# Sixty-four of 128 rows of an adaLN product moved from the merge, projection and FFN stages into the gate units

## What is computed

```python
shift_mix, scale_mix, gate_mix, shift_ffn, scale_ffn, gate_ffn = jnp.split(
    silu_c @ w_ada[l] + b_ada[l], N_ADA, axis=-1)
...
h_x = modulate(x, norm_mix[l], shift_mix, scale_mix)
p_x = h_x @ w_in[l]
u_x, hy_x, gates_x = jnp.split(p_x, [S5_WIDTH, S5_WIDTH + 3 * HY_WIDTH], axis=-1)
y_x = (s5_readout(s5_states(u_x, lp, 0, st_ctx_f[:, -1], False), lp, 0)
       + s5_readout(s5_states(u_x, lp, 1, st_ctx_b[:, 0], True), lp, 1))
x = x + gate_mix[:, None] * mixer_output(u_x, y_x, hy_x, gates_x, lp)
x = x + gate_ffn[:, None] * swiglu(modulate(x, norm_ffn[l], shift_ffn, scale_ffn),
                                   w_ffn_in[l], w_ffn_out[l])
...
return rms_norm(x, norm_f)
```

## Time and profile before

| quantity | value |
|---|---|
| median of 3 runs | 2881.26 us (2880.14 to 2881.98) |
| span of the profiled execution | 2886.0 us |
| busy: PE, PEld, DVE | 2822.8, 2456.8, 1939.7 us |
| busy: ACT, POOL | 970.0, 272.1 us |
| gate units 10 to 31 | about 665 to 968 us |
| spectrum, merge, output projection | about 968, 1130 and 1311 us on, to 1474 us |
| FFN with its pairs, down projection | about 1482 to 2382 us, to 2866 us |

### The profile page before, as it was taken

One profiled execution on the slowest core, in us unless ns is written; L12 is line 12 of the kernel. 1 busy time (PEld: TensorE's weight loads), 2 busy tenths in 40 slices (PEclk: granted clock), 3 DMA queues, 4 the chain that ended last, 5 costly groups with the idle time before them and its releaser, 6 DMA issues.

```text
span 2886.0 us, 40851 instructions
## 1 busy us (share of the span) xinstructions
PE 2822.8 (98%) x17044; PEld 2456.8 (85%) x17044; DVE 1939.7 (67%) x2657; ACT 970.0 (34%) x1376; POOL 272.1 (9%) x475
## 2 busy tenths in 40 slices
PE   7999999999999999999989999999999999999997
PEld 2688788888888888887879999999999997888886
DVE  6546666985543777887768888888888774343445
ACT  4332333224442532221154444444443442222221
POOL 0001331001223001111100000000000000000000
PEclk9999999999999999999999999999999999999998
DMA  9726974334445537886544444444443335434333
GB/s 403 294 92 150 189 182 141 119 121 134 133 129 173 200 132 255 291 287 249 205 157 150 143 147 141 148 139 149 140 143 111 121 129 193 137 99 136 96 100 109
DMA packets 139531, 473.73 MB, mean 164 GB/s; under 512 B 24417, under 2 KB 24673, under 8 KB 134610
## 3 DMA queue, kind: packets, MB, share of 16 engines
q1 hardware_dynamic: 84226, 302.96, 31.8%
q0 software_dynamic: 47248, 156.09, 16.8%
q10 hardware_dynamic: 7872, 12.06, 1.2%
HBM read 426.53 MB, written 44.43 MB: 163 GB/s over the span
## 4 chain that ended last, share of the span: by engine, by line
PE 90%; DMA 4%; DVE 3%; ACT 2%; issue 1%; POOL 0%; ACTq 0%; DVEq 0%; SPq 0%; POOLq 0%
PE ps L2048 11%; PE ps L2050 10%; PE ps L2049 10%; PE ps L2303 10%; PE ps L2304 10%; PE ps L2305 10%; PE ps L2333 5%; PE ps L2334 5%; PE ps L2335 5%; DMA hw_raw<-in_w_in 2%; PE ps L2065 2%; PE ps L2018 1%; PE ps L2127 1%; DMA hw_raw<-in_w_out 1%; PE ps L2066 1%; PE ps L1959 1%
## 5 line engine op out<-in xcount | busy, mean ns | idle before, releaser
L1124 DVE TENSOR_TENSOR hw_lo<-hw_raw,hw_hi 128x1024 fp32r<-128x1024 f32 (+1 forms) x348 | 382.7, 1101 | 629.7 <-ACT hw_hi L680 628.0
L680 ACT ACTIVATE hw_hi<-hw_raw 128x1024 fp32r<-128x1024 f32 (+1 forms) x348 | 333.7, 961 | 1049.1 <-DMA hw_raw<-in_w_in 469.0
L1050 ACT ACTIVATE wx_hi<-wx 128x1024 fp32r<-128x1024 f32 x287 | 303.5, 1058 | 445.9 <-PE ps L2305 431.6
L1771 DVE TENSOR_TENSOR wx_lo<-wx,wx_hi 128x1024 fp32r<-128x1024 f32 x287 | 350.4, 1222 | 58.8 <-ACT wx_hi L1050 58.7
L2303 PE MATMUL ps<-t_hi,wx_hi 128*128 128x256 f32 x1312 | 371.3, 283 | 0.0
L2304 PE MATMUL ps<-t_lo,wx_hi 128*128 128x256 f32 x1312 | 371.3, 283 | 0.0
L2305 PE MATMUL ps<-t_hi,wx_lo 128*128 128x256 f32 x1312 | 371.3, 283 | 0.0
L2048 PE MATMUL ps<-h_hi,hw_hi 128*128 128x512 f32 x896 | 354.4, 396 | 3.7 <-DVE st_b L1389 2.6
L2050 PE MATMUL ps<-h_hi,hw_lo 128*128 128x512 f32 x896 | 350.6, 391 | 0.0
L2049 PE MATMUL ps<-h_lo,hw_hi 128*128 128x512 f32 x896 | 350.4, 391 | 0.0
L2303 PE MATMUL ps<-h_hi,wx_hi 128*128 128x256 f32 x984 | 278.6, 283 | 0.0
(11 more groups left out here) (359 smaller groups left out, 5187.6 us busy)
## 6 DMA issues: line engine op xcount, KB each, us to landing
wx<-in_w_fi SPq DMA_DIRECT2D x164, 512.0 KB, 3.3
hw_raw<-in_w_in SPq DMA_DIRECT2D x128, 512.0 KB, 4.2
ada1m<-in_w_ar POOLq DMA_DIRECT2D x128, 512.0 KB, 4.8
ada_mix<-in_w_ac SPq DMA_DIRECT2D x16, 2048.0 KB, 12.7
hw_raw<-in_w_fo SPq DMA_DIRECT2D x64, 384.0 KB, 3.1
hw_raw<-in_w_fo SPq DMA_DIRECT2D x64, 320.0 KB, 2.9
hw_raw<-in_w_glu SPq DMA_DIRECT2D x32, 512.0 KB, 4.8
hw_raw<-in_w_out SPq DMA_DIRECT2D x32, 512.0 KB, 4.4
```

What stands on the lines that cost most here:

```text
L680: act.activation(hw_hi[slot(n)][:, 0:width(n)], hw_raw[slot(n)][:, 0:width(n)], ACT.Copy).then_inc(w_hi, 1)
L1124: tt(hw_lo[s][:, 0:w], hw_raw[s][:, 0:w], hw_hi[s][:, 0:w].bitcast(F32), SUB).then_inc(w_lo, 1)
L1771: tt(wx_lo[o % 12][:, :], wx[o % 12][:, :], wx_hi[o % 4][:, :].bitcast(F32), SUB).then_inc(w_lo, 1)
```

## The change

Rows 0 to 63 (groups 0 to 3) are now added up in gate units 10 to 28, in the place of the first chunks of the S5 states, which nobody reads any more after the scan. They have three load buffers `ada1g` in place of four, and an accumulator in two pieces of 512 columns, so each row is two DVE instructions. Units 10 to 13 take four rows each, 14 to 17, 19 to 22 and 24 to 27 three, 18, 23 and 28 four. The sums over partitions of groups 0 to 3 stand on TensorE after H0 of units 14, 19, 24 and 29. Rows 64 to 127 stay in the merge (3 a full tile, 1 a filling tile, 36 in all) and in the output projection (2 a tile, 28 in all). The FFN has none.

```diff
-N_WIDE = 96
+N_GATE = 64
...
+    ada1g = [at(f"ada1g_{j}", 126 + 4 * j, [P, 1024]) for j in range(3)]
+    accg = [at(f"accg{j}", (138, 180)[j], [P, 512]) for j in range(2)]
...
+    def gate_rows(g):
+
+        if g < P3 or g >= P3 + 19:
+            return range(0)
+        if g < P3 + 4:
+            return range(4 * (g - P3), 4 * (g - P3) + 4)
+        q, i = (g - P3 - 4) // 5, (g - P3 - 4) % 5
+        return range(16 * q + 16 + 3 * i, 16 * q + 16 + (3 * i + 3 if i < 4 else 16))
...
             def ada_in(r):
 
-                if r >= 4:
-                    pool.wait_ge(ada1_used, r - (3 if r < N_WIDE + 2 else 1))
-                pool.dma_start(ada1m[row_slot(r)][:, :], w_ar_d[r]).then_inc(ada1_in[row_slot(r)], 16)
+                if 3 <= r < N_GATE:
+                    pool.wait_ge(ada1_used, r - 2)
+                if r >= N_GATE + 4:
+                    pool.wait_ge(ada1_used, r - 3)
+                pool.dma_start(row_buffer(r)[:, :], w_ar_d[r]).then_inc(ada1_in[row_slot(r)], 16)
...
+            pool.wait_ge(rec_dn, 1)
+            for r in range(3):
+                ada_in(r)
+            for r in gate_rows(P3):
+                ada_in(r + 3)
             for t in range(NS):
                 toeplitz(t)
+                for r in gate_rows(P3 + 1 + t):
+                    ada_in(r + 3)
                 if t == 9:
                     store_y(0)
+            for g in range(P3 + 1 + NS, P3 + 19):
+                for r in gate_rows(g):
+                    if r + 3 < N_GATE:
+                        ada_in(r + 3)
...
             store_y(1)
+            pool.wait_ge(ada1_used, N_GATE)
+            pool.wait_ge(acc1_red, 4)
             for s in range(2):
                 pool.dma_start(tf_raw[:, s, :, :], ...
...
@@ DVE, gate unit g
                 if 0 <= g - P3 - 2 < NS:
                     outputs(g - P3 - 2)
+                if g in (P3 + 4, P3 + 9, P3 + 14, P3 + 19):
+                    ada_mod((g - P3 - 4) // 5, ps[2])
+                for r in gate_rows(g)[:2]:
+                    ada_row(r)
...
                     readout_table(g - P3, 1)
+                for r in gate_rows(g)[2:]:
+                    ada_row(r)
...
@@ DVE, merge and output projection
-                last = row + (5 if full and i < 14 else 4 if full else 2)
+                last = row + (3 if full else 1)
...
-                last = min(row + (3 if m < 10 else 2), N_WIDE)
+                last = min(row + 2, N_ROW)
...
@@ PE, gate unit g
                 half_unit(2 * u, ps[u % 2][:, :], h_hi, h_lo, 0, True, False)
+                if g in (P3 + 4, P3 + 9, P3 + 14, P3 + 19):
+                    ada_columns((g - P3 - 4) // 5, ps[2])
                 if 0 <= g - P3 - 1 < NS:
                     lags(g - P3 - 1)
```

More of the change, by code:

```diff
@@ L38 @@
 N_ADA0 = 32
+N_ROW = 128
 HU = 1024
@@ L363, in row_slot, with row_buffer @@
     def row_slot(r):
-        return r % 4 if r < N_WIDE else r % 2
+        return r % 3 if r < N_GATE else r % 4
+    def row_buffer(r):
+        return (ada1g if r < N_GATE else ada1m)[row_slot(r)]
+    def gate_rows(g):
[5 more added lines that the diff above has]
+        return range(16 * q + 16 + 3 * i, 16 * q + 16 + (3 * i + 3 if i < 4 else 16))
     def row_loads(r):
@@ L627, in _ @@
             pool.wait_ge(pq_ps, 8)
-            for r in range(62):
-                if 2 <= r < 4:
-                    pool.wait_ge(yv, 5 + r)
+            for r in range(N_GATE, 100):
+                if N_GATE + 2 <= r < N_GATE + 4:
+                    pool.wait_ge(yv, 5 + r - N_GATE)
                 ada_in(r)
@@ L635, in _ @@
                 pool.dma_start(xacc[:, 4 * g:4 * g + 4, :], x_d[:, 4 * g:4 * g + 4, :]).then_inc(xa_in[g], 16)
-                for r in range((62, 68, 80, 92)[g], (68, 80, 92, N_WIDE)[g]):
+                for r in range((100, 104, 112, 120)[g], (104, 112, 120, N_ROW)[g]):
                     ada_in(r)
@@ L639, in _ @@
             pool.dma_start(xs_d, xacc[:, :, :]).then_inc(xs_out, 16)
-            for r in range(N_WIDE, N_WIDE + 2):
-                ada_in(r)
             def store_act(g):
@@ L914, in _ @@
                     transposed_u(0)
+                    act.wait_ge(acc1_red, 4)
                     gelu_hi(0)
@@ L1344, in ada_row @@
                 dve.wait_ge(ada1_in[row_slot(r)], 16 * row_loads(r))
-                a = accm[g % 2][:, :]
-                if k == 0:
-                    if g >= 2:
-                        dve.wait_ge(acc1_red, g - 1)
-                    ins = ts(a, ada1m[row_slot(r)][:, :], silu_c[:, k:k + 1, 0], None, MUL)
-                else:
-                    dve.wait_ge(ada1_used, r)
-                    ins = stt(a, ada1m[row_slot(r)][:, :], silu_c[:, k:k + 1, 0], a, MUL, ADD)
+                if k == 0 and (1 <= g < 4 or g >= 6):
+                    dve.wait_ge(acc1_red, g if g < 4 else g - 1)
+                if k:
+                    dve.wait_ge(ada1_used, r)
+                w = row_buffer(r)
+                accs = ([(accg[c][:, :], slice(512 * c, 512 * c + 512)) for c in range(2)] if r < N_GATE
+                        else [(accm[g % 2][:, :], slice(0, 1024))])
+                for a, cols in accs:
+                    if k == 0:
+                        ins = ts(a, w[:, cols], silu_c[:, k:k + 1, 0], None, MUL)
+                    else:
+                        ins = stt(a, w[:, cols], silu_c[:, k:k + 1, 0], a, MUL, ADD)
                 ins.then_inc(ada1_used, 1)
@@ L1643, in _ @@
                 row = last
-                if i in (7, 11):
-                    ada_mod((i - 7) // 4, ps[6])
+                if i == 11:
+                    ada_mod(4, ps[6])
                 if full:
@@ L2035, in ada_columns @@
                 for j in range(8):
-                    ins = mm(bank[:, 400 + 8 * (g % 2) + j:401 + 8 * (g % 2) + j], accm[g % 2][:, P * j:P * j + P],
-                             ones[:, 0:1], start=True, stop=True)
+                    acc = accg[j // 4][:, P * (j % 4):P * (j % 4) + P] if g < 4 else accm[g % 2][:, P * j:P * j + P]
+                    ins = mm(bank[:, 400 + 8 * (g % 2) + j:401 + 8 * (g % 2) + j], acc, ones[:, 0:1], start=True, stop=True)
                 ins.then_inc(acc1_red, 1)
@@ L2209, in _ @@
                 b = 3 * (m % 2)
-                if i in (6, 10):
+                if i == 10:
                     pe.wait_ge(cv_out, 8)
-                    ada_columns((i - 6) // 4, ps[6])
+                    ada_columns(4, ps[6])
                 if m < N_FILL:
@@ L2230, in _ @@
                 if m == 1:
-                    ada_columns(2, ps[0])
-                if m == 5:
-                    pe.wait_ge(acc1_mod, 3)
-                    ada_columns(3, ps[0])
-                if m == 10:
-                    pe.wait_ge(acc1_mod, 4)
-                    ada_columns(4, ps[0])
+                    ada_columns(5, ps[0])
+                if m == 8:
+                    pe.wait_ge(acc1_mod, 6)
+                    ada_columns(6, ps[0])
                 if m == 15:
-                    pe.wait_ge(acc1_mod, 5)
-                    ada_columns(5, ps[0])
+                    pe.wait_ge(acc1_mod, 7)
+                    ada_columns(7, ps[0])
                 each = (m_lo, PLACE) if m == 0 else None
@@ L2256, in _ @@
             rstd_tokens(2)
-            pe.wait_ge(acc1_mod, 6)
+            pe.wait_ge(acc1_mod, 8)
             for j in range(4):
@@ L2312, in _ @@
                     pe.wait_ge(wz_free, p - 1)
-                if p in (17, 33):
-                    if p == 33:
-                        pe.wait_ge(acc1_mod, 7)
-                    ada_columns((p - 1) // 16 + 5, ps[4 * ((p + 1) % 2) + 3])
                 for j in range(7):
```

16 lines of the change are left out of this document (5 added, 11 removed).

## The result

The changed kernel takes 2926.27 us, the median of 5 runs (2920.83 to 2937.72), against 2881.26 us, also of 5 (2876.34 to 2885.3). The ratio is 1.0153, with a 95% interval of 1.0137 to 1.0169. The profiled execution of the changed kernel has a span of 2924.5 us and a mean granted clock of 0.983; the one before had 2886.0 and 0.991.

The account below looks back on a forecast made before the run. TensorE bounds it, busy 2822.8 of 2886.0 us; DVE costs only where TensorE waits. Terms 9.6 + 7.5 + 6.7 + 10.2 + 2 - 4.3 - 4.8 = 26.9 us on 2881.3 gave 2908 us, range 2886 to 2928.

Parts of the forecast that it names:

- forecast case: Whole kernel: waits for sums and the half clock make it slower, 2908 us, own range 2893 to 2924; chance 0.62.
- shared engines: Rival, gate units: row loads slow SP's weights from 4.3 to 7.2 us landing; +15 us, 2923; chance 0.15.
- 1.4 that would vanish: Unit 19: its existing 1.4 us wait is swallowed by the longer wait before it; with 3.4 of half clock, -4.8.
- The half clock: After three sum waits: TensorE loses 3.4 us each to the 1.2 GHz clock, 10.2 us (bounds 0 and 17).
- spectrum stage: Spectrum's start: POOL's loads (`tf_raw`, `uh`, `y_st`) go out 16.5 us late, delaying ACT's GELU; 2 us (bounds 0 and 7).
- Sums waiting for row d: Units 19 and 24: TensorE waits 4.8 us each for the preceding unit's fourth row, 9.6 us; unit 14's sum 6.7.
- The 64 small matmuls are moved, not added: Row groups' sums on TensorE: moving them to the gate units was put at no cost in the sum.
- unit 28 has no tables left: Sum in unit 29: no wait for the fourth row, unlike units 18 and 23; put at nothing.
- Units 11 to 13: Cold start with four rows each: small waits at lags, tables and outputs, 7.5 us (bounds 3 and 12).
- three-row units: Gate units with three rows: rows end at 794.5, before the outputs at 797.2, so they cost TensorE nothing.
- The lost waits of merge and projection: Merge and output projection: fewer rows there remove all 4.3 us of TensorE's waits, -4.3.
- A shorter FFN: FFN: its rows are hidden already, removing them gives 0, length about 900 us; a shorter one would mean being wrong.

Follow-up runs that it names:

- holds ahead of the lags: Kernel before, with TensorE held ahead of the lags in units 14, 19 and 24 until VectorE made four additional operations: 2905.82 us, ratio 1.0082.
- additions-only kernel: Changed kernel without the loads of gate rows 3 to 63, all 64 additions made from what lies in the buffers: 2897.49 us, ratio 1.0044.
- load experiments: Changed kernel without loads of gate rows 3 to 63: 2897.49 us; these cut to 64 columns: 2907.46; full loads without 60 rows' additions: 2908.37.
- early row load: Changed kernel with the load into the first row's buffer issued ahead of the four Toeplitz loads in each gate unit: 2932.8 us, ratio 1.0165.
- the spectrum's loads issued early: Changed kernel with sums behind the chunk outputs and `tf_raw`, `y_st` and first filter spectra loads ahead of the `acc1_red` 4 wait: 2908.75 us, ratio 1.0087.
- the holds of 1.5 to 4.5 us: Kernel before, with TensorE held behind the chunk outputs: in five units, 2908.53 us; in units 14, 19 and 24 by seven additional VectorE operations, 2897.96 us.

## Why the prediction was right in kind and 18 us low

The measured 2926.3 us lies 2 us above the forecast case's own upper bound (2924); it is inside the full range only because that reached up past the shared engines. The waits in the gate units were right as a total: 23.8 us were forecast, less 1.4 that would vanish, and 22.0 came. That is in part luck, since the terms were off both ways. The half clock was not right: 10.2 less 3.4 were forecast, 6.8 us, and 26.9 came. These 20 us are more than the whole error. The sums in the gate units add 6 and the spectrum stage 1.4; the stages after it gave back 8.4 more than forecast.

**Sums waiting for row d: right.** 4.8 us in units 19 and 24 was forecast, and the three waits were 4.4 to 4.8; the issue behind the Toeplitz loads was as forecast. In unit 14 it was 4.6, not 6.7: counted from the first lags, row 15 ended 1.0 us earlier than forecast and TensorE came 1.2 us later. A row took 1.46 us (2.92 for two) where I had 1.6. The landing that I took, 5.6 us, lies between the 4.6 of row d in unit 18 (806.38 to 811.0) and the gate units' median of 6.4:

```profile
DMA to landing us min/median/max: 3.5/6.4/9.6
```

**The half clock: the mis-sized term.** This is the step that failed by the most. I took 3.4 us for each of three sums from the earlier trace rows, and they were 6.3 to 6.7: 9.3 us too little. The row was of a 1.4 us wait with no sum behind it. The holds ahead of the lags show 5 us behind a wait of 4.3, so a price from the wait's length alone would have found half of that. The additions-only kernel shows that a waiting sum adds to it: 3.4 to 5.1 us lost behind a wait of 1.5, where the earlier trace rows has 3.4. And I priced no other fall of the clock in the gate units, where there were four: 4.2 us of work behind the Toeplitz wait of unit 12, 3.2 at unit 29's sum, and 1.7 each at 839 and 955 us. My upper bound for this term, 17 us, lies below the 19.5 of the three sums.

**"The 64 small matmuls are moved, not added": wrong in the clock.** The groups by form show them with their price (count | busy us, mean ns | idle before). In the changed kernel:

```profile
L2071 PE MATMUL ps<-ones,accg 128*128 128x1 f32 x64 | 14.3, 353 | 17.2 <-DVE accg L1384 17.2
L2071 PE MATMUL ps<-ones,accm 128*128 128x1 f32 x64 | 7.4, 245 | 0.0
```

In the kernel before all eight sums have 14.7 us:

```profile
L2036 PE MATMUL ps<-ones,accm 128*128 128x1 f32 x128 | 14.7, 245 | 0.0
```

A sum is 1.8 us of TensorE at full clock and 3.6 where it now stands. At full clock the move is neutral, but it explains the stage table: two sums left the FFN's pairs, two left merge and projection, four came into the gate units.

**Unit 29: a wait that was put at nothing.** I wrote that unit 28 has no tables left and shows no wait. Its sum waited 3.4 us. VectorE's timeline there:

```profile
971.64 1.23 DVE L1152 TENSOR_TENSOR hw_lo<-hw_raw,hw_hi 128x1024 fp32r<-128x1024 f32 x1 [9.35 <-ACT hw_hi L707]
972.78 2.93 DVE L1384 SCALAR_TENSOR_TENSOR accg<-ada1g,silu_c,accg 128x512 f32<-128x512 f32 x4
...
981.44 1.41 DVE L1384 SCALAR_TENSOR_TENSOR accg<-ada1g,silu_c,accg 128x512 f32<-128x512 f32 x2 [3.27 <-DMA ada1g<-in_w_ar]
```

Tables were beside the point. Row d's load waits for row a, row a for the unit's first split, and that split came late, at 971.64. With the wait of 3.4 us went 3.2 of clock and the sum's own 1.8; another 1.7 are the fall at 955 us, and 0.8 a wait at the chunk outputs. That is the 11.1 us of that stretch.

**Units 11 to 13.** I had 7.5 us of small waits at lags, tables and outputs; there was one, 4.3 us for the first Toeplitz tile, behind row 7's load. The clock behind it is what I had left out (0.53 over the 11 us from 689, with 1.8 us of the wait in it, so 4.2 us of work):

```profile
689.00:700.00 11.00, 9.09 (x35) 8.32 (x36) 6.07 (x10) 4.49 (x9) 0.99 (x2) 0.53 0.57 210
```

**The shared DMA engines: partly true.** This rival had 7.2 us for the weights' landing and 15 us. In the changed kernel the weights of the gate units landed after 5.3 us, before after 4.3:

```profile
DMA to landing us min/median/max: 3.6/5.3/9.5
```

It showed at the Toeplitz tiles of units 20 and 21 (two waits, 2.5 us in all, with 1.7 us of clock; 3.7 us in the stage table), which I had at nothing, since I held three-row units to be free. The load experiments agree: the bytes cost more than the additions. The Trainium skill (DMA: Bandwidth & Descriptors, on queues and rings), cited there, says that an engine takes turns between the queues' rings. The trace agrees in kind: beside an early row load the Toeplitz loads took 5.1 us in place of 3.6. No run here separates that rule from a mere lack of bandwidth.

**The rest.** The lost waits of merge and projection were right (0.3 us left of 4.3). The stages gave back 9.9 us in all: 4.0 for these, 3.7 for the two sums that left, and 2.2 that I have not traced. The spectrum stage took 3.4 us for a forecast of 2, by another wait than forecast. `tf_raw` went out 17.2 us ahead of the transposes (987.07 to 1004.23), where 15.4 were forecast, so that step was right. The GELU idled 4.80 us for `y_st`, and TensorE then waited 2.4 us for the odd part; with the spectrum's loads issued early that wait was 0.2. The FFN's additions gave nothing, as forecast: the 2.8 us of the last line are, within a microsecond, the two sums that left the pairs (3.7). A shorter FFN was to be a sign of being wrong; these two sums, which I had overlooked there, explain it.

## What to carry to other kernels

Before you move work that a busy engine must wait for, ask of its last piece, not of the mean: which buffer its load needs, when that is freed, and what stands ahead of it in the queue. Putting the consumer 2 to 3 us later, behind work that TensorE has anyway, was worth 13.7 us by the medians (ratio 1.0101 in place of 1.0153); putting the load earlier was worth nothing, because its neighbours paid. And price a wait on TensorE by a row from the same place, not by its length alone. Ahead of small matmuls count it about twice: behind the holds of 4.0 to 4.3 us the clock took another 4.6 to 5.1. Behind them the price did not grow with the length: the holds of 1.5 to 4.5 us cost another 1.6 to 3.0. To find the price in a trace, multiply the time at half clock by one half, but leave out the part in which the engine stood still.
